# Gates of the second block's mixers: products over 256 normalised columns instead of 258 unnormalised ones

## What is computed

```python
for l in range(DEPTH):
    sh1, sc1, g1, sh2, sc2, g2 = modulation(c, l)
    h = rms_norm(x, ln1_g[l]) * (1.0 + sc1) + sh1
    z = h @ w_in[l]
    u_pool, c_q_raw, c_kv_raw, k_rope_raw, gz_a, gz_b = jnp.split(z, cuts, axis=-1)
    y_a = pool_mixer(u_pool, w_pool[l], pool_scale[l]) @ p_pool[l]
    y_b = mla(c_q_raw, c_kv_raw, k_rope_raw, ...) @ p_attn[l]
    merged = sigmoid(gz_a) * y_a + sigmoid(gz_b) * y_b
    x = x + g1 * (merged @ w_out[l])
    h2 = rms_norm(x, ln2_g[l]) * (1.0 + sc2) + sh2
    x = x + g2 * (square(relu(h2 @ w_ff1[l])) @ w_ff2[l])
```

## Time and profile before

| | us |
|---|---|
| median of 3 runs | 1823.88 |
| lowest, highest | 1823.15, 1823.88 |
| the profiled execution's own time | 1823.08 |
| its span, first to last instruction | 1821.7 |
| TensorE busy | 1809.8 (99%) |
| VectorE busy | 1353.6 (74%) |
| ScalarE busy | 1047.8 (58%) |

### The profile page before, as it was taken

One profiled execution on the slowest core, in us unless ns is written; L12 is line 12 of the kernel. 1 busy time (PEld: TensorE's weight loads), 2 busy tenths in 40 slices (PEclk: granted clock), 3 DMA queues, 4 the chain that ended last, 5 costly groups with the idle time before them and its releaser, 6 DMA issues.

```text
span 1821.7 us, 36563 instructions
## 1 busy us (share of the span) xinstructions
PE 1809.8 (99%) x15035; PEld 1777.6 (98%) x15035; DVE 1353.6 (74%) x2332; ACT 1047.8 (58%) x1751; POOL 3.1 (0%) x9
## 2 busy tenths in 40 slices
PE   9999999999999999999999999999999999999998
PEld 9999999999999999999899999999999999999998
DVE  7787786677876778778677887797976559788654
ACT  6454675665444545467656455676665458666533
POOL 0000000000000000000000000000000000000000
PEclk9999999999999999999999999999999999999999
DMA  8886443467785678644357888455566655566663
GB/s 311 293 281 239 128 142 103 133 194 252 261 306 180 216 270 293 216 131 148 105 162 224 284 281 282 133 185 151 167 204 186 187 177 171 160 174 187 189 192 106
DMA packets 92566, 364.59 MB, mean 200 GB/s; under 512 B 11148, under 2 KB 12076, under 8 KB 86256
## 3 DMA queue, kind: packets, MB, share of 16 engines
q1 hardware_dynamic: 91968, 361.46, 62.3%
q10 hardware_dynamic: 432, 0.79, 0.1%
HBM read 361.15 MB, written 1.05 MB: 199 GB/s over the span
## 4 chain that ended last, share of the span: by engine, by line
PE 91%; DVE 6%; ACT 2%; issue 1%; DMA 0%; SPq 0%; DVEq 0%; ACTq 0%
PE bank L582 27%; PE bank L584 27%; PE bank L583 27%; PE bank L642 2%; DVE w_lo L1788 1%; PE bank L639 1%; PE bank L638 1%; PE bank L864 1%; ACT w_hi L1217 1%; PE bank L879 1%; PE bank L909 0%; DVE s_pool L2315 0%; PE bank L816 0%; PE bank L1045 0%; DVE gates L2391 0%
## 5 line engine op out<-in xcount | busy, mean ns | idle before, releaser
L582 PE MATMUL bank<-xn_hi,w_hi 128*128 128x272 f32 (+2 forms) x2256 | 650.6, 288 | 0.3 <-DVE w_lo L1788 0.3
L584 PE MATMUL bank<-xn_lo,w_hi 128*128 128x272 f32 (+2 forms) x2256 | 641.3, 284 | 0.0
L583 PE MATMUL bank<-xn_hi,w_lo 128*128 128x272 f32 (+2 forms) x2256 | 641.0, 284 | 0.0
L1788 DVE TENSOR_TENSOR w_lo<-raw_b,w_hi 128x1024 fp32r<-128x1024 f32 (+3 forms) x280 | 353.4, 1262 | 151.5 <-ACT w_hi L1217 149.2
L1788 DVE TENSOR_TENSOR w_lo<-raw_a,w_hi 128x1024 fp32r<-128x1024 f32 (+1 forms) x276 | 348.8, 1265 | 143.4 <-ACT w_hi L1217 142.2
L1217 ACT ACTIVATE w_hi<-raw_a 128x1024 fp32r<-128x1024 f32 (+2 forms) x278 | 301.9, 1086 | 265.8 <-PE bank L584 255.3
L1217 ACT ACTIVATE w_hi<-raw_b 128x1024 fp32r<-128x1024 f32 (+3 forms) x280 | 304.9, 1089 | 255.9 <-PE bank L584 251.2
L582 PEld LDWEIGHTS bank<-xn_hi,w_hi 128*128 128x128 f32 x2256 | 425.8, 189 | 7.9 <-issue 6.0
L583 PEld LDWEIGHTS bank<-xn_hi,w_lo 128*128 128x128 f32 x2256 | 425.8, 189 | 0.7
L584 PEld LDWEIGHTS bank<-xn_lo,w_hi 128*128 128x128 f32 x2256 | 425.8, 189 | 0.0
L582 PE MATMUL bank<-h_hi,w_hi 128*128 128x272 f32 (+1 forms) x704 | 200.8, 285 | 0.0
(11 more groups left out here) (368 smaller groups left out, 3143.5 us busy)
## 6 DMA issues: line engine op xcount, KB each, us to landing
raw_b<-in_weights SPq DMA_DIRECT2D x244, 512.0 KB, 3.7
raw_a<-in_weights SPq DMA_DIRECT2D x240, 512.0 KB, 3.7
ada_raw<-in_ada_w SPq DMA_DIRECT2D x48, 1024.0 KB, 4.9
raw_a<-in_weights SPq DMA_DIRECT2D x32, 704.0 KB, 5.3
raw_b<-in_weights SPq DMA_DIRECT2D x32, 704.0 KB, 5.4
raw_b<-in_weights SPq DMA_DIRECT2D x6, 256.0 KB, 4.5
c_rows<-in_c_rows SPq DMA_DIRECT2D x3, 512.0 KB, 4.4
raw_a<-in_weights SPq DMA_DIRECT2D x4, 384.0 KB, 3.2
```

The source lines that it names most:

```text
L582: pe.matmul(o, wh, xh, start=start, stop=False)
L583: pe.matmul(o, wl, xh, start=False, stop=False)
L584: return pe.matmul(o, wh, xl, start=False, stop=stop)
L1788: dve.tensor_tensor(lo, raw_of(c, u), hi.bitcast(F32), ALU.subtract).then_inc(*k.up("w_lo"))
```

## The change

The mixers' 16 gates take `z_hi`, `z_lo` of 256 columns too (`MIX_SCALED` = 10). The tiles are made during the first steps: `z_scale` of tile 0 stands behind the norm, and each step of the three engines' programs makes one tile, ScalarE's `z_high` ahead of the step's other work and VectorE's `z_low` behind the step's `w_lo`. `early_z(l)` says how many tiles are made before step 0: none in layer 0, two in layer 1. TensorE waits for the last tile before the first gate. The gates' `scaled_tile` is gone; ScalarE's Tanh reads the bank and needs no bias. To make room, `scores`, `pt2` and `a2` move from their own place into that of `xn`, which is not read after step 9, and z keeps the place that it has in `ff`. The scratch of `z_scale` in the mixer is `s_pool`, so `pooled` waits for the last z tile before it clears it.

```diff
--- before.py
+++ after.py
@@ -228,7 +228,9 @@
             return tuple(sb(name + part, [P, tiles, width], F32R, 256, 224 if width == N else past) for part, past in (("_hi", 0), ("_lo", 128)))
 
         self.x = sb("x", [P, KD, T])
+        xn_at = place
         self.xn_hi, self.xn_lo = streamed("xn", KD)
+        xn_end = place
         self.sumsq, self.sq, self.sq2 = (sb(n, [P, T]) for n in ("sumsq", "sq", "sq2"))
 
         self.sq_pair = nc.alloc_sbuf_tensor_at("sq_pair", [P, 2, T], F32, offset=place - 4 * 2 * T)
@@ -298,6 +300,7 @@
         self.f_hi, self.f_lo = streamed("f", KF2, N)
 
         self.xg = sb("xg", [P, KD, N])
+        z_at = place
         self.z_hi, self.z_lo = streamed("z", KD, N)
         assert place <= end - 8 * N - 64
         place = shared
@@ -317,10 +320,13 @@
         self.k_rot = sb("k_rot", [96, N])
         self.q_all, self.k_all = sb("q_all", [96, MH, N]), sb("k_all", [96, MH, N])
         self.v_tok, self.r_tmp = sb("v_tok", [P, 2, 512]), sb("r_tmp", [P, N])
-        self.scores, self.pt2, self.stat2 = sb("scores", [P, 2, 3 * P]), sb("pt2", [P, 4, 3 * P]), sb("stat2", [P, 32])
+        self.stat2 = sb("stat2", [P, 32])
+        assert place <= z_at
+
+        place = xn_at
+        self.scores, self.pt2 = sb("scores", [P, 2, 3 * P]), sb("pt2", [P, 4, 3 * P])
         self.a2_hi, self.a2_lo = streamed("a2", 4, N)
-
-        assert place <= end - 8 * N - 64
+        assert place <= xn_end
         place = latent
         self.y2_hi, self.y2_lo = streamed("y2", KD, N)
 
@@ -351,7 +357,7 @@
     return 4 + b if i % 2 and b < 2 else b
 
 
-FF_SCALED = 8
+FF_SCALED, MIX_SCALED = 8, 10
 
 
 def is_moved(at):
@@ -434,6 +440,11 @@
 def both_ways(c, j):
 
     return (c.full, c.gate)[j][:, 0, :]
+
+
+def early_z(l):
+
+    return 2 * l
 
 
 def z_shift(c, stage, kk):
@@ -1136,9 +1147,13 @@
             if is_moved(at):
                 if at == 5:
                     rope_keys(u, b, l)
+                elif at >= MIX_SCALED:
+                    if at == MIX_SCALED:
+                        pe.wait_ge(*k.at("x_lo", ("z", *stage, KD - 1)))
+                    tile(u, b, TN, c.z_hi, c.z_lo)
                 elif at > 3:
                     tile(u, b, TX, *streams(c, stage))
-                free[b] = [("tile_v", ("n2", l, at))]
+                free[b] = [("tile_v", ("n2", l, at)) if at < MIX_SCALED else ("tile_a", ("gate", l, gate_of(at)))]
             elif at in (12, 13):
                 queries(u, at - 12, l)
                 if at == 13:
@@ -1646,17 +1661,24 @@
         squares = [c.sq2[:, 0:N], c.gate[:, 0, 0:N], c.gate[:, 1, 0:N], c.sq[:, 0:N], c.full[:, 0, 0:N]]
         chains = [(3, 12, latent(l, "cq", 3, QL, c.cq, c.cq_hi)), (5, 13, latent(l, "ckv", 2, KVL, c.ckv, c.ckv_hi)),
                   (6, 12, k_rope(l)), (9, 14, pooled(l)), (17, 35, attention2(l))]
+        for kk in range(early_z(l)):
+            z_high(stage, kk)
         u = u0
         for at in range(47):
             finish(chains, at)
             if at < 39:
                 split_hi(u + 4)
+            if at + early_z(l) < KD:
+                z_high(stage, at + early_z(l))
             if at == 9:
                 load_table(EXP_TANH_SET)
             elif at == 41:
                 load_table(LN_EXP_SET)
             if is_moved(at):
-                act.wait_ge(*k.at("tile_v", ("n2", l, at)))
+                if at < MIX_SCALED:
+                    act.wait_ge(*k.at("tile_v", ("n2", l, at)))
+                else:
+                    act.wait_ge(k.sem["unit_done"], u + 1)
                 if at < 5:
                     name, kk, t = ("cq", at, c.cq_x) if at < 3 else ("ckv", at - 3, c.ckv_x)
                     s = t[:, kk, N:N + 1]
@@ -1671,7 +1693,7 @@
                 else:
 
                     j = gate_of(at)
-                    act.activation(c.gates2[:, j, :], c.gates2[:, j, :], ACT.Tanh, bias=c.gates2_x[:, j, N + 1:N + 2], scale=0.5).then_inc(*k.up("tile_a", ("gate", l, j)))
+                    act.activation(c.gates2[:, j, :], bank[moved_bank(at)][:, 0:N], ACT.Tanh, scale=0.5).then_inc(*k.up("tile_a", ("gate", l, j)))
                 if 22 < at < 27:
                     g = at - 23
                     act.wait_ge(*k.at("tile_a", ("pw", l, g)))
@@ -1868,8 +1890,6 @@
 
     def z_low(stage, kk):
 
-        if kk == 0:
-            z_scale(stage, 0)
         if kk + 1 < KD:
             if kk:
                 dve.wait_ge(*k.at("x_lo", ("z", *stage, kk - 1)))
@@ -2298,6 +2318,7 @@
 
     def pooled(l):
 
+        dve.wait_ge(*k.at("x_lo", ("z", "ln1", l, KD - 1)))
         for b in (c.u_pool, c.s_pool):
             dve.memset(b[:, :, 0:META], 0.0).then_inc(*k.up("pooled"))
         for at in range(7):
@@ -2357,6 +2378,9 @@
         chains = [(5, 13, latent(l, "ckv", 2, c.sq[:, 0:N], [c.full[:, 0, 0:N]], c.ckv, c.ckv_hi, c.ckv_lo, V_KVG)),
                   (3, 12, latent(l, "cq", 3, c.sq2[:, 0:N], [c.gate[:, 0, 0:N], c.gate[:, 1, 0:N]], c.cq, c.cq_hi, c.cq_lo, V_QG)),
                   (6, 13, k_rope(l)), (8, 15, pooled(l)), (13, 15, q_rope(l)), (17, 35, attention2(l))]
+        z_scale(stage, 0)
+        for kk in range(early_z(l)):
+            z_low(stage, kk)
         u = u0
         for at in range(47):
             finish(chains, at)
@@ -2366,8 +2390,6 @@
                 scaled_tile(u, c.full[0:64, 1, TX], 5, ("n2", l, at), rows=64)
             elif at < 10:
                 scaled_tile(u, c.u_pool[:, at - 6, META:T + 2], moved_bank(at), ("n2", l, at))
-            elif is_moved(at):
-                scaled_tile(u, c.gates2_x[:, gate_of(at), :], moved_bank(at), ("n2", l, at))
             if l == 0 and 26 < at < 31:
                 in_place(TB, c.vg[:, G_FN:G_FN + 8], c.rstd2[:, :], "fn", range(2 * at - 54, 2 * at - 52))
                 if at == 30:
@@ -2401,6 +2423,8 @@
                 u += 1
             if at < 46:
                 split_lo(u + 4)
+            if at + early_z(l) < KD:
+                z_low(stage, at + early_z(l))
             if at >= 39:
                 add_squares(m, TB, ("ff", l))
                 if m == 0:
```

## The result

The changed kernel takes **1827.92 us** (median of 14 runs, 1827.03 to 1833.64), the kernel before 1823.79 beside it (14 runs, 1823.09 to 1825.26). The ratio is 1.0023, 95% interval 1.0016 to 1.0030: slower by 0.23%, or 4.1 us, just beyond the 0.2% that counted as no change; the interval takes in both sides of that bound. The forecast was 1825.4, inside a range of 1820.4 to 1828.4. The profiled execution of the changed kernel took 1828.19 us against 1823.08, 5.1 more. TensorE stood 1.0 us later than before already when the second block's first mixer began (1164.72 against 1163.70), ahead of anything the change touches; the other 4.1 us arise behind that.

What follows compares the result with a forecast made beforehand. TensorE's stream and the waits put into it were taken as the bound. Layer 0 at +2.2 and layer 1 at +0.1 made +2.3 us on the profiled 1823.08, so 1825.4 us; stated range 1820.4 to 1828.4.

Steps and rivals of the forecast that it cites:

- What bounds it: Whole kernel: TensorE busy 99% of the span, so only its time per matmul and waits put into its stream count.
- The products: Gates of both layers: 32 units go from 2.88 to 2.80 us, a gain of 2.56 us, all on the path.
- rival 3: Gate units: two columns cost only their streaming, so 1.9 us of the gain are missing, 1827.3 us; chance 0.06.
- Work on VectorE, layer 0: Steps 0 to 7: 6.4 us added, 3.1 absorbed by waits, VectorE 3.3 us late, 2.9 before the last z_low.
- The wait at unit 10: First gate of layer 0: TensorE stands still 3.6 us for z tile 7, any delay by the latents' sums included.
- Layer 0: +3.6 - 0.16 - 16 x 0.08 = +2.2 us: Layer 0's sum: new wait at unit 10, less the present wait at unit 17, less 16 shorter gate units.
- the old wait: Layer 0, unit 17: TensorE's present wait of 0.16 us for w_lo, expected to go.
- Layer 1: No wait at unit 10; 1.2 us lost at unit 17's w_lo, 1.12 regained by 14 units behind: +0.1 us.
- Rival 2: Steps 0 to 7, both layers: VectorE and ScalarE hold each other up; slower from 1827.5 us on; chance 0.12.
- Rival 1: New VectorE work is hidden, z tile 7 comes in time: 1820.2 us, or 1820 to 1823 if partly; chance 0.24.
- the forecast's own: The forecast's own range for the whole kernel, 1823.4 to 1827.5 us, with unused VectorE waits its softest number.
- The top of the bounds: Both layers with none of VectorE's waits used: layer 0 +5.1 us, layer 1 +2.8, together 1831.0 us.

Runs made afterwards that it cites:

- the products alone: Kernel before with its 16 gates a layer over 256 columns of xn, no z tile made, normalisation and shift left out: 1821.64 us, ratio 0.9989.
- the pause was filled: Changed kernel with 30 unused matmuls on z tile 0 ahead of layer 0's wait for z tile 7: 1826.20 us, ratio 1.0014.
- the split wait: Changed kernel, but the first gate's unit waits for each z tile only ahead of that tile's three matmuls: 1826.39 us, ratio 1.0017.
- the two GpSimd kernels: Changed kernel with z made on GpSimd, ScalarE copying the high part: 1831.35 us; the same with VectorE making the low part: 1829.60 us.
- the shorter pause: Kernel before, TensorE held before unit 10 of layer 0 until the w_lo of unit 12, no z made: 1827.90 us, ratio 1.0022.
- the pause of 5.71 us: Kernel before, TensorE held before unit 10 of layer 0 until the w_lo of unit 13, no z made: 1831.45 us, ratio 1.0042.

## Why the prediction was right, and where it was not

- **What bounds it.** Right as far as it goes. TensorE's stream and the waits in it explain what was seen, once its clock, which the forecast left out, is added; and the page's 74% for VectorE said nothing on steps 0 to 17, where work beyond its waits is not hidden.
- **The products.** Forecast 0.08 us a unit, and 0.085 in the trace of the changed kernel. The choice between 0.08 and 0.02 us a unit was right, and rival 3, which had the rule of the Trainium skill's page, is settled against that rule. The -2.5 us of the products alone is no second proof of the 2.56: its trace has 0.05 us a unit, and 0.4 us of its gain comes from stalls at unit 16 that are gone.
- **Work on VectorE, layer 0.** Forecast 3.1 of 3.5 us of its waits used. The trace of the changed kernel still has waits of 0.9 (for `cq_hi`) and 0.5 (for `w_hi`) on VectorE there, where 0.4 were to be left; yet the last `w_lo` is 3.3 us late and not 2.9, a miss of only 0.4. The instructions start 0.40 us apart as forecast, 15 of them or 6.0 us ahead of this `w_lo`, so 2.7 us were taken up, where the brackets fell by only 2.2 (3.5 - 1.3). The rest is idle time that no bracket counts: from the first eviction to the split behind it there were 0.49 us before (1167.49 to 1167.98), and 0.34 now.
- **The wait at unit 10.** Forecast 3.6, measured 3.64. That is partly luck: z was 0.4 us later than forecast, and TensorE came 0.46 us later too, because the latents' sum held it up. The prediction held this "part of the 3.6, not on top of it"; it was on top.
- **The step that failed** is the line "Layer 0: +3.6 - 0.16 - 16 x 0.08 = +2.2 us". It prices a pause at its length, and lets the units behind it run at their usual 2.80 us: the term for the clock is missing, put at nothing without a reason. The first took 4.24 us and the next 3.01, since the granted clock fell: 1.65 us by the offsets, and 1.7 by the medians when the pause was filled. The Trainium skill, page "TensorE: Matmul & The Clock Gate", section "Part 1: The HAM clock gate", has an idle TensorE fall back to its half-speed level, and activity release it from there. The trace of the changed kernel agrees with that (0.50 behind the pause, 1.00 from 1202.09 on). The prediction should have had it as a term, or a rival, once its own sum contained a pause of this length. With the 0.46 of the sum, it is 2.1 us against the 1.7 by which layer 0 was missed; the other steps give 0.4 back, nearly all of it at units 16 and 17, where the forecast counted 0.16 us for the old wait and 0.51 came back.
- **Layer 1.** Forecast +0.1, measured 0.0 when made alone (+0.3 by its offsets) and +0.2 in the trace of the changed kernel. The mechanism was right, the place was not: the wait of 0.97 us is at unit 14, not at unit 17, whose wait stays at 0.17.
- **The rivals.** Rival 2 forecast slower by this much, through waits of VectorE that would go unused. Its time of 1828.3 is nearly the measured one, but not its cause: VectorE is 0.4 us later than in the forecast, and what carries the time over the bound is the clock. Rival 1 was far off. Without the clock the forecast's sum is good to 0.4 us (+2.3 against +2.0 by the medians and +2.65 by the offsets with the wait filled).
- **The range and the chances.** The measured time lies inside the stated range and outside the forecast's own, which ended at 1827.5. It is inside because the range took in part of rivals 2 and 3, not because the forecast foresaw the clock; this is luck. So is the small distance to the 0.2% bound: "within" had 0.81 and slower 0.14, and the ratio came out 0.03% beyond. The top of the bounds is a little low: with none of the 5.8 us used the time is 1825.4 + 5.8 = 1831.2 us, not 1831.0.

Open: what decides whether the clock falls behind a given pause, and why 256 columns of z go quicker than 256 of xn. By the medians the split wait costs 0.7 us more than the filled one; the traces do not show this difference, since their offsets agree (2.65 us both), and the intervals overlap.

## What to carry to other kernels

A pause in TensorE's stream is not paid by its length alone: look at the granted clock behind it, and if a wait of some 2 to 4 us cannot be avoided, split it by tile, put work in it, or move the deadline; each gave back 1.0 to 1.7 us here by the medians (0.8 to 1.5 by the offsets). Price added work on a helper engine where that engine has waits in the very steps concerned, then follow its lateness to the next place without margin: moving the deadline only moves the bill. Test the gain and the cost as two kernels, one with each; here -2.5 and +5.5 us showed where the loss lies, which the sum of +4.1 could not. And read small differences from offsets within the traces: the -2.5 turned out to be 1.6 of products and 0.4 of stalls that were gone.

## What the runs showed of the hardware

- The clock fell to its lower level behind pauses of 2.97, 3.64 and 5.71 us in layer 0, and behind pauses of 2.74 and 2.29 us in layer 1 of the two GpSimd kernels. It did not fall behind pauses of 1.19, 2.74 and 2.92 us in layer 0. (These are gaps between starts, less a spacing; the brackets are 0.16 us less.) So length alone does not decide: 2.29 us brought it down and 2.92 us did not, in the same execution. The window behind the 2.92:

```profile
1196.00:1198.00 2.00, 2.00 (x20) 2.00 (x19) 1.93 (x6) 1.94 (x5) 0.00 (x0) 1.00 0.92 256
```

- Each fall cost 1.6 to 1.9 us on top of the pause, whatever its length (offsets behind the five pauses).
- The fall can come after TensorE has begun again: 1.3 us after it in the changed kernel (1194.84 to 1196.11) and in the shorter pause (1193.05 to 1194.40), 0.4 us behind the pause of 2.29 us. In the pause of 5.71 us it came before. A reader who looks only at the idle window sees 1.00 in the changed kernel.
- Two columns fewer than 258 saved 2.1 ns a matmul with the operand left as it was, and 3.5 ns with the z tiles in its place, where the rows of 256 and 272 columns give 0.83 ns for two.
- VectorE, where it reads two tiles of SBUF, and GpSimd slow each other: a split on VectorE goes from 1.22 to 1.75 us, a product on GpSimd from 0.81 to 1.60.
